# Ten of the sixteen late modulation groups on VectorE, two row sums side by side in column tiles

## The reference

```
def adaln(cond, w_mod, b_mod):
    m = jax.nn.silu(cond) @ w_mod + b_mod
    return m.reshape(cond.shape[0], N_MOD, D_MODEL)
```

## Time and profile before

| | us |
|---|---|
| median of 3 runs | 4627.2 |
| lowest and highest | 4626.64, 4640.03 |
| the profiled execution, as timed | 4624.79 |
| its span in the trace | 4623.0 |

### The profile page before, as it was taken

One profiled execution on the slowest core, in us unless ns is written; L12 is line 12 of the kernel. 1 busy time (PEld: TensorE's weight loads), 2 busy tenths in 40 slices (PEclk: granted clock), 3 DMA queues, 4 the chain that ended last, 5 costly groups with the idle time before them and its releaser, 6 DMA issues.

```text
span 4623.0 us, 60331 instructions
## 1 busy us (share of the span) xinstructions
PE 4462.3 (97%) x25249; PEld 3285.4 (71%) x25249; DVE 3094.3 (67%) x4135; ACT 593.3 (13%) x1161; POOL 1482.4 (32%) x1047
## 2 busy tenths in 40 slices
PE   7989999999999998999999999999999999999997
PEld 2776446445885444466555445799999999999997
DVE  1455518897997774247777587978855558886556
ACT  1530001432431000000000010100000000000001
POOL 0110002673334643103544244433322223322221
PEclk8999999999999999999999999999999999999999
DMA  9939988995448989987999987599999999999998
GB/s 396 405 124 379 375 336 348 390 409 233 140 142 313 408 350 408 385 334 304 421 420 420 411 317 298 225 377 419 419 420 419 408 406 421 418 420 418 403 420 334
DMA packets 237322, 1663.40 MB, mean 360 GB/s; under 512 B 28230, under 2 KB 32728, under 8 KB 37786
## 3 DMA queue, kind: packets, MB, share of 16 engines
q0 software_dynamic: 129616, 936.57, 49.9%
q1 hardware_dynamic: 99348, 677.25, 36.6%
q10 hardware_dynamic: 8088, 45.73, 2.5%
HBM read 1639.68 MB, written 18.94 MB: 359 GB/s over the span
## 4 chain that ended last, share of the span: by engine, by line
PE 39%; DMA 8%; DVE 7%; issue 1%; POOL 1%; ACT 0%; ACTq 0%; DVEq 0%; POOLq 0%
PE ps L249 26%; PE ps L2737 12%; DMA arena_sb<-peer_v,arena_sb 7%; DVE arena_sb L447 3%; PE ps L2679 1%; POOL arena_sb L396 0%; DMA x_rows<-arena_sb 0%; DVE arena_sb L2426 0%; DVE arena_sb L2436 0%; DVE arena_sb L2428 0%; DVE arena_sb L2433 0%; DVE arena_sb L2423 0%; DVE arena_sb L2509 0%; DVE arena_sb L2464 0%; DVE arena_sb L2455 0%
## 5 line engine op out<-in xcount | busy, mean ns | idle before, releaser
L249 PE MATMUL ps<-arena_sb 128*128 128x224 f32 (+3 forms) x9728 | 2292.8, 396 | 8.4 <-ACT arena_sb L2237 2.6
L249 PEld LDWEIGHTS ps<-arena_sb 128*128 128x128 f32 x9728 | 1670.7, 192 | 614.2 <-issue 327.8
L447 DVE SCALAR_TENSOR_TENSOR arena_sb<-arena_sb 128x2048 f32<-128x2048 f32 x412 | 986.6, 2395 | 473.8 <-DMA arena_sb<-peer_v,arena_sb 442.9
L442 DVE CUSTOM_DVE_ANT_0 arena_sb<-arena_sb 128x2048 f32<-128x2048 f32 x416 | 975.5, 2359 | 326.7 <-DMA arena_sb<-peer_u,arena_sb 326.5
L396 POOL DMA_INDIRECT arena_sb<-peer_v,arena_sb x416 | 606.9, 1459 | 1135.6 <-DVE arena_sb L447 929.4
L396 POOL DMA_INDIRECT arena_sb<-peer_u,arena_sb x416 | 628.6, 1511 | 924.1 <-DVE arena_sb L442 571.6
L2737 PE MATMUL ps<-arena_sb 128*128 128x224 f32 x4096 | 776.5, 353 | 1.3 <-ACT arena_sb L2776 0.7
L2737 PEld LDWEIGHTS ps<-arena_sb 128*128 128x128 f32 x4096 | 774.4, 190 | 2.2 <-issue 1.0
L1949 PE MATMUL ps<-arena_sb 128*128 128x512 f32 x768 | 338.7, 599 | 15.0 <-DMA arena_sb<-w_gb_r 7.4
L1949 PEld LDWEIGHTS ps<-arena_sb 128*128 128x128 f32 x768 | 144.7, 191 | 203.4 <-issue 181.3
L2132 PE MATMUL ps<-arena_sb 128*128 128x512 f32 x640 | 275.8, 593 | 3.1 <-DMA arena_sb<-w_out 1.9
(11 more groups left out here) (329 smaller groups left out, 2871.4 us busy)
## 6 DMA issues: line engine op xcount, KB each, us to landing
arena_sb<-peer_ut SPq DMA_DIRECT2D x128, 1024.0 KB, 9.3
arena_sb<-peer_vt SPq DMA_DIRECT2D x128, 1024.0 KB, 9.3
arena_sb<-w_mod POOLq DMA_DIRECT2D x61, 1024.0 KB, 9.3
arena_sb<-w_qkv SPq DMA_DIRECT2D x48, 1024.0 KB, 9.2
arena_sb<-w_out SPq DMA_DIRECT2D x48, 1024.0 KB, 6.9
arena_sb<-w_query SPq DMA_DIRECT2D x48, 1024.0 KB, 7.1
arena_sb<-w_mod SPq DMA_DIRECT2D x35, 1024.0 KB, 8.9
arena_sb<-w_ga_r SPq DMA_DIRECT2D x32, 1024.0 KB, 8.4
```

Source lines behind the costliest of these rows:

```text
L249: mm = pe.matmul(out, weights[:, k * P:(k + 1) * P], x[:, k, :], start=(k == 0), stop=(k == chunks - 1))
L442: nc.vector.tensor_tensor_reduce(rows, rows, total, 1.0, 0.0, ALU.mult, ALU.add, seg.dots[:, p:p + 1]).then_inc(t.rows_used, 1)
L447: nc.vector.scalar_tensor_tensor(out=total, in0=rows, scalar=seg.weight[:, p:p + 1], in1=total, op0=ALU.mult, op1=ALU.add).then_inc(t.rows ...
```

## The change

- M_VECTOR is now groups 2 to 11, ten of them. TensorE keeps 0, 1 and 12 to 15.
- The heads take 16 `w_mod` tiles (groups 0 to 3). A table, MOD_TILES, mixes the order so that two TensorE tiles are followed by one VectorE tile, and MOD_HEADS says behind which weight tile each is done: VectorE's behind tiles 2, 5, 8, 11 (group 2) and 14, 17, 19, 21 (group 3). Row sums follow in the heads behind tiles 6, 12 and 14.
- The recurrence takes group 4: its first tile in one piece ahead of the first `differences`, the other three cut into twelve quarters of two instructions (`mod_quarter`) at the head of the levels 1 to 5 of each scan, one in each, two in level 5.
- `branches` takes groups 5 to 7 with the same number of tiles as before, and the sums of groups 3 and 4 in its w_z part. `merge_one` takes 16 tiles (groups 8 to 11) and not 12; two of the four more come ahead of its first product, the other two in its last chunk. Its last row sum stands ahead of the last `turn`.
- A row sum of a VectorE group is two matmuls with 32 columns of ones, one in column tile 0 and one in column tile 32, so that the two rows lie in partitions 0 and 32. Bias, addition and store take 33 partitions, of which the store reads two.
- Four sets of accumulators in place of two (MOD_SETS), and a semaphore of its own for VectorE's tiles (`mod_added`).

```diff
-M_VECTOR = range(6, 12)
+M_VECTOR = range(2, 12)
+MOD_TILES = (0, 1, 8, 2, 3, 9, 4, 5, 10, 6, 7, 11, *range(12, 4 * M_REST))
+MOD_HEADS = (0, 1, 2, 3, 4, 5, 6, 7, 8, 9, 10, 11, 14, 17, 19, 21)
...
+def mod_quarter(dve, nc, t, m, j):
+
+    n, kq = divmod(MOD_TILES[m], 4)
+    if j == 0:
+        mod_landed(dve, t, m)
+        if kq:
+            after(dve, t.mod_added, MOD_TILES[m] - 4 * M_VECTOR.start)
...
+def mod_sum(pe, t, n):
+
+    after(pe, t.mod_row, n)
+    if n in M_VECTOR:
+        pe.wait_ge(t.mod_added, 4 * (n + 1 - M_VECTOR.start))
         for c in range(2):
...
-        pe.matmul(t.ps[0:2, 7, :], t.of_cond[0], t.mod_acc[n % 2][0], start=True, stop=False)
-        pe.matmul(t.ps[0:2, 7, :], t.of_cond[1], t.mod_acc[n % 2][1], start=False, stop=True).then_inc(t.mod_summed, 1)
+            mm = pe.matmul(t.ps[32 * c:32 * c + 32, 7, :], t.ones[:, 0:32], t.mod_acc[MOD_SETS[n]][c], start=True,
+                           stop=True, tile_position=(0, 32 * c))
...
@@ -880,9 +923,10 @@
             if ctx:
-                if n % 4 == 1 and n > 4:
-                    mod_sum(pe, t, n // 4 - 1)
-                mod_tile(pe, t, n)
+                if n in summed_at:
+                    mod_sum(pe, t, summed_at.index(n))
+                if n in MOD_HEADS and not by_vector(MOD_HEADS.index(n)):
+                    mod_tile(pe, t, MOD_HEADS.index(n))
...
@@ -927,12 +969,14 @@
+                if n in MOD_HEADS and by_vector(MOD_HEADS.index(n)):
+                    mod_products(dve, nc, t, MOD_HEADS.index(n))
...
         def level(n, r, k):
+            if ctx and k < LEVELS - 1:
+                i = 5 * n + k - 1
+                for m, j in quarters[sum(between[:i]):sum(between[:i + 1])]:
+                    mod_quarter(dve, nc, t, m0 + m, j)
...
         if ctx:
+            mod_products(dve, nc, t, m0)
             dve.wait_ge(t.gates, 8)
...
@@ -1954,6 +2013,8 @@
                 if ctx and s == (2 if c else 3):
                     mod_sum(pe, t, m0 // 4 - 1 + c)
+        if ctx:
+            mod_sum(pe, t, m0 // 4 + 3)
         turn(3)
```

175 lines of the change are left out of this document (102 added, 73 removed).

## The result

| | before | after |
|---|---|---|
| median of the runs, same chip | 4627.2 (11 runs) | 4644.0 (10 runs) |
| the profiled execution, as timed | 4624.79 | 4651.09 |
| its span in the trace | 4623.0 | 4649.3 |

The ratio after/before is 1.0031, with a 95% interval from 1.0021 to 1.004. On another chip, beside 27 runs of the kernel before, it was 1.0031 again (1.002 to 1.0041). An eleventh run after took 13213.74 us, in another state of the chip, and is left out. The medians lie 16.8 us apart, and the ratio puts the loss at 14 us (0.0031 of 4627). I had forecast 4627.5, with a range up to 4638.

What follows compares the result with a forecast made beforehand. TensorE's order was taken to set the pace in the heads, with DMA near its end and VectorE free. Terms from -16.4 to +4.5 us summed to +0.3 us, so a median of 4627.5 us, range 4617 to 4638.

Steps and rivals of the forecast that it cites:

- Heads, off TensorE: In the heads, 15 fewer `w_mod` tiles and two fewer row sums on TensorE up to the last projection: -16.4 us.
- Heads, the norm chain: In the heads, VectorE's products delay the squares that TensorE's norm sums need: +4.5 us, bounds 0 and 9.
- Gate chain: End of the heads: TensorE waits at `cumsums` behind VectorE's products and convolutions, +3.9 us, bounds 0 and 5.5.
- clock: Last projection of the heads may run at half speed after TensorE's wait: +1.8 us, bounds 0 and +3.7.
- Start of the recurrence: First differences wait for group 4's first tile on VectorE, +2.6 us; first products partly at half clock, +1 us.
- levels: Recurrence scans: VectorE's quarters exceed its idle time at level 5 of both scans, +3.1 us, bounds 0.5 and 5.
- Branches: w_z part: two more row sums, +0.6 us; w_u part: two sums in cheaper form, twice -0.9; together -1.2 us.
- Row sums and merge: Merge: four cheaper row sums and a fifth, -2.0 us; four more tile loads, +3 us, bounds 0 and 10.6.
- The rivals: Four cases: VectorE's work hidden (chance 0.1), late tiles (0.07), merge choking on DMA (0.12), row-sum pair not overlapping (0.05).
- Late tiles hold VectorE: Heads: VectorE's tiles land only at 13 us, holding VectorE and TensorE: +20 us, 4648, chance 0.07.
- The rule of the Trainium skill: Heads: VectorE's two-port mode locks memory for GpSimd's descriptors, delaying loads; room for 0.4 us, no term of the sum.

## Why the prediction was wrong

The forecast was that nothing would be gained or lost (+0.3 us); by the marks it is +11.6 in one profile and +8.1 in another, and +14 by the ratio. In the marks' stages (the decays now start 1.4 us behind the last projection and not 3.0, so 1.6 us go from the heads to the recurrence):

| us | forecast | first profile | second |
|---|---|---|---|
| heads | -7.8 | -0.7 | +1.0 |
| recurrence | +8.3 | +7.6 | +4.7 |
| `branches` | -1.2 | -0.5 | -1.9 |
| merge and output projection | +1.0 | +5.2 | +4.4 |

So the heads are the larger part of the miss, the merge with the output projection the smaller. The steps in turn:

**Heads, off TensorE, -16.4.** Right. The stage before had 24 `w_mod` tiles and the one after 8, and TensorE's busy time in the window fell by 13.2 us. That is the 16.4, 1.8 more for the tile and the sum that stood behind the last projection, less 5.3 that the matmuls at the lower clock took longer (1.7, 0.9 and 2.7, below).

**Heads, the norm chain, +4.5.** Too large: 1.6 us in four waits of 0.74 or less. The convolution of a tile that is followed by products, and the next one:

```profile
139.00 0.35 DVE L948 TENSOR_SCALAR arena_sb<-ps,cw_sb 128x128 f32<-128x128 f32 x1 [2.62 <-PE ps L252]
...
146.05 0.34 DVE L948 TENSOR_SCALAR arena_sb<-ps,cw_sb 128x128 f32<-128x128 f32 x1
```

They are 7.05 us apart, where my sum of 2.4 and 5.5 gave 7.9. Most of it is the tile: the first of a group has two shorter instructions (L312) among its eight and took 4.8 us. The other tiles' eight took 5.38, and starts lie a little closer than durations add up. So the wait behind tile 2 was 0.16 and not 1.0.

**The step that failed: a term at nothing, between the norm chain and the gate chain.** The prediction counted what VectorE does for TensorE in units of convolution, normalise and products, and the row sums only as time on TensorE. It left out the chain of a group's finish: row sum, bias, store, the next group's bias. The bias on VectorE waits for the landing of the store before, and the store stands in GpSimd's list behind a load that now waits for VectorE. It spoke of GpSimd's list only for how soon a tile lands. The price: 4.3 us of wait, 1.7 in the two projections and 0.9 in the gate sums at the lower clock, 6.9 in all. It made the next terms larger too: with the store moved, the heads gained 9.8. The forecast wrote "about 118" for the stage from 127, but its own terms give 119.5 (127.3 less 7.8). It was 126.6; with the store moved it was 117, less than 119.5 because the norm chain had been taken 2.9 too large.

**Gate chain, +3.9, and clock, +1.8.** The wait was 4.4 (3.3 with the store moved): right in size. The last projection lost 2.7 where I took 1.8 of a possible 3.7. The reason given for the wait was half right. In the experiment with the gate products first, VectorE's tile was no longer in the way, and ScalarE's functions held TensorE for 2.0 instead.

**Start of the recurrence, +2.6 and +1; levels, +3.1.** The sum is 6.7, or 8.3 by the marks, against 7.6 and 4.7 in the two profiles. The first differences start 5.9 us behind the last projection (248.95 to 254.87) and not 6.85, again because the first tile of a group is the shorter one. The mechanism is what the runs show: filling VectorE's gap with the first tile gave 3.6, freeing level 5 of the first scan brought the recurrence from 94.1 to 87.8. But a level's quarter was not priced for the clock: with the early store, where the clock fell behind the wait, 6.3 us went and not 2.4.

**Branches, -1.2.** -0.5 by the marks; the two new sums alone, without the two sums more in the w_z part, gave -1.9. Both are near what one profile's marks can tell.

**Row sums and merge, -2.0 and +3.** The new sum takes 0.98 to 0.99 us against 0.9 forecast: right. The merge and the output projection are longer by 3.5 and 1.7, against +1. The four extra loads cost 4.0 us of waits for weights instead of 3. The last sum waits 2.1 for the bias, where I had 0.67, but most of that wait is old. Before, the last turn stood at the same place for VectorE's last addition:

```profile
PE ps L1935 <- DVE arena_sb L2003: 1.5, 1, 1.5
```

From the end of the merge's products to the output projection it was 2.0 us and is 3.6, so the fifth sum cost the 1.6 that I had (0.67 and 0.9). The four sums' gain is the part that came out small: with the new sums alone the merge fell by 2.0 us and not by four times 0.9. These are single profiles, and how the remaining us divide is open. The output projection's 1.7 is not traced to a row of its own; it was 0.2 to 1.8 in all the kernels built on the changed one, and -0.1 with the new sums alone.

**The rivals.** None of them came. *Late tiles hold VectorE* had nearly the right price (4648), by luck: VectorE waited for a store and never for a tile, and TensorE for one load. The loads in the heads after, median to landing:

```profile
arena_sb<-w_mod POOLq DMA_DIRECT2D x16, 1024.0 KB, 8.6
```

It was 9.1. In the second profile of the changed kernel it is 9.7, so it is not shown that landings got shorter, as I had argued.

**The range** held only what I had in the sum. A stage in which TensorE, VectorE, ScalarE and GpSimd each wait for one another needed a rival of the form "a wait I haven't listed", and the width of the interval should have come from the whole 16.4 us that this stage stood to gain.

**The rule of the Trainium skill** that the prediction weighed, on GpSimd's descriptors and VectorE's two-port mode, is not seen: the load instruction on GpSimd takes 542 ns in the mean of the changed kernel and 543 in that of the kernel before (from the rows of this line in their pages). What bears on this case is a plainer sentence. The timeline shows GpSimd's store of a finished row ten us late behind its own load's wait. The Trainium skill says, in "DMA: Bandwidth & Descriptors", section "Anatomy of one DMA — SWDGE (gpsimd) path", that DMA engines don't wait for semaphores and that the wait happens on the issuing sequencer, and in "PSUM — Partial Sum Buffer", section "Engine vs sequencer instructions", that GpSimd's queue is strict FIFO; the traces agree: the load waits 13.28 us before it is issued, and the store goes out 0.52 us behind it.

## What to carry to other kernels

When a resource changes hands between two engines, list for every in-order queue that releases or refills it what stands behind the new wait: a 4 KB store queued behind a load held VectorE for 8.9 us, and through it ScalarE and TensorE. Put what is ready early (stores, bias loads) ahead of what waits late. Then look for the receiving engine's own idle stretches and put the new work there, not at the head of a phase: the same tile cost 3.6 us in front of the differences and nothing in the gap of 6.4 us six us earlier.
